# Differential attention on one core: scores two heads ahead, values one head behind, VectorE's work in a new order

## The reference, cut to what matters

```python
sc = jnp.einsum('bqhcd,bkhcd->bhcqk', qb, k)
p = jax.nn.softmax(sc, axis=-1)
a = p[:, :, 0] - lam_full * p[:, :, 1]
out = jnp.einsum('bhqk,bkhe->bqhe', a, v)
```

## Time and profile before

| | |
|---|---|
| Median of three runs | 3047.74 us (3039.37 to 3050.79) |
| The profiled execution | 3042.34 us |
| Its span in the trace | 3040.7 us |
| Granted clock of TensorE, mean | 0.917 of 2.4 GHz |
| TensorE matmul busy | 2671.5 us, 88% of the span |
| VectorE busy | 783.5 us, 26% |
| ScalarE busy | 336.9 us, 11% |
| GpSimd busy | 29.7 us, 1% |
| Moved by DMA | 729.65 MB, mean 240 GB/s |

### The profile page before, as it was taken

How to read it: one execution, slowest core, us unless ns; L and a number is a source line. 1 busy time by engine, 2 the same in 40 slices (tenths; PEclk the granted TensorE clock), 3 DMA queues, 4 the chain that set the end, 5 groups by cost and what they waited for, 6 DMA issues and landing times. The chain is left out here.

```text
span 3040.7 us, 28745 instructions
## 1 busy us (share of the span) xinstructions
PE 2671.5 (88%) x10935; PEld 1588.9 (52%) x10936; DVE 783.5 (26%) x1801; ACT 336.9 (11%) x663; POOL 29.7 (1%) x48
## 2 busy tenths in 40 slices
PE   6977699999997999968999799959998996957998
PEld 3433333333332333337787477647767774734775
DVE  1222322212121221232832243234441001232001
ACT  2111011111111111110122000010001000021000
POOL 0000000000000000000000000000000000000000
PEclk8967699999999999989999899969997997967999
DMA  7600599999998899966323477347963545102443
GB/s 296 242 0 2 229 419 428 428 429 428 428 428 342 349 428 428 428 265 234 139 100 149 152 288 260 111 148 259 354 225 132 166 154 196 57 1 83 152 136 105
DMA packets 188107, 729.65 MB, mean 240 GB/s; under 512 B 9343, under 2 KB 102877, under 8 KB 159381
## 3 DMA queue, kind: packets, MB, share of 16 engines
q1 hardware_dynamic: 169044, 653.41, 54.7%
q0 software_dynamic: 19008, 75.50, 6.5%
HBM read 727.83 MB, written 1.05 MB: 240 GB/s over the span
## 5 line engine op out<-in xcount | busy, mean ns | idle before, releaser
L2132 PE MATMUL bank<-hT,ffn_wgu 128*128 128x256 f32 x2816 | 622.3, 382 | 29.1 <-DMA ffn_wgu<-in_ffn_w_gu 25.8
L2132 PEld LDWEIGHTS bank<-hT,ffn_wgu 128*128 128x128 f32 x2816 | 538.7, 192 | 123.1 <-issue 42.8
L1387 PE MATMUL bank<-experts_raw,tiled_xs 128*64 128x512 f32 x2112 | 474.3, 599 | 17.4 <-DMA experts_raw<-in_w_up 13.6
L1387 PEld LDWEIGHTS bank<-experts_raw,tiled_xs 128*64 128x64 f32 x2112 | 147.8, 138 | 333.3 <-issue 295.1
L2146 PE MATMUL bank<-ffn_wd,ffn_actT 128*128 128x512 f32 x704 | 308.6, 592 | 0.0
L1387 PE MATMUL bank<-experts_raw,tiled_act_s 128*64 128x512 f32 x1056 | 241.0, 602 | 48.4 <-DMA experts_raw<-in_w_down 47.1
L1714 PE MATMUL bank<-hT,second_ring 128*128 128x256 f32 x1024 | 226.1, 384 | 17.2 <-DMA second_ring<-in_w_in 17.2
L1714 PEld LDWEIGHTS bank<-hT,second_ring 128*128 128x128 f32 x1024 | 197.4, 193 | 46.1 <-issue 18.5
L2195 DVE TENSOR_TENSOR ffn_actT<-ffn_silu,bank 128x256 f32<-128x256 f32 x88 | 36.9, 421 | 694.1 <-ACT ffn_silu L2175 694.1
L2146 PEld LDWEIGHTS bank<-ffn_wd,ffn_actT 128*128 128x128 f32 x704 | 133.8, 190 | 151.3 <-issue 149.2
L1387 PEld LDWEIGHTS bank<-experts_raw,tiled_act_s 128*64 128x64 f32 x1056 | 71.3, 137 | 196.1 <-issue 123.5
(11 more groups left out here) (460 smaller groups left out, 1974.2 us busy)
## 6 DMA issues: line engine op xcount, KB each, us to landing
experts_raw<-in_w_gate SPq DMA_DIRECT2D x64, 2048.0 KB, 23.7
experts_raw<-in_w_up SPq DMA_DIRECT2D x64, 2048.0 KB, 25.1
experts_raw<-in_w_down SPq DMA_DIRECT2D x64, 2048.0 KB, 25.5
ffn_wgu<-in_ffn_w_gu SPq DMA_DIRECT2D x88, 1024.0 KB, 9.8
ffn_side_w<-in_mod_w POOLq DMA_DIRECT2D x30, 2048.0 KB, 12.0
ffn_wd<-in_ffn_w_down SPq DMA_DIRECT2D x44, 1024.0 KB, 5.2
second_ring<-in_w_in SPq DMA_DIRECT2D x16, 2048.0 KB, 7.7
mla_wm<-in_w_mod SPq DMA_DIRECT2D x24, 1024.0 KB, 6.4
```

The source lines that it names most:

```text
L1387: last = nc.tensor.matmul(bank[b][h * HALF:(h + 1) * HALF, :], stationary(kt), raw[p][:, k, h * C:(h + 1) * C], start=kt == 0, stop=kt == ...
L2132: last = nc.tensor.matmul(bank[b][:, m * SEQ:(m + 1) * SEQ], wgu[:, s, m, k, f * P:(f + 1) * P], core.hT[:, k, :], start=k == 0, stop=k == ...
```

## The change

TensorE makes the scores of head h+2 before the transposes of head h, and the value product of head h-1 after them; `attend` is split into `turn_prob` and `attend`. On VectorE `finish` loses its copy of the output, which becomes `take_o`; the maxima of head h+2 come behind the finish of head h, and the copy of head h-2 between them. ScalarE's list is unchanged.

```diff
--- before.py
+++ after.py
@@ -2393,7 +2393,7 @@
                                                 qk[64 * c:64 * c + 64, KT + h, :], start=True, stop=True)
                     last.then_inc(*core.filled[b].up())
 
-            def attend(h):
+            def turn_prob(h):
                 b = 4 + h % 2
                 pe.wait_ge(*S["prob_ready"].next(pe, TT))
                 core.claim(pe, b)
@@ -2402,7 +2402,9 @@
                         last = nc.tensor.transpose(bank[b][:, c * SEQ + t * P:c * SEQ + (t + 1) * P],
                                                    prob[h % 2][:, t, 0, c * P:(c + 1) * P], core.ident[:])
                 last.then_inc(*core.filled[b].up())
-                core.copied(pe, b)
+
+            def attend(h):
+                core.copied(pe, 4 + h % 2)
                 b = 6 + h % 2
                 core.claim(pe, b)
                 for t in range(TT):
@@ -2414,10 +2416,14 @@
             pe.wait_ge(*S["turned"].next(pe, KT))
             core.copied(pe, 6, 7)
             scores(0)
+            scores(1)
             for h in range(H3):
-                if h + 1 < H3:
-                    scores(h + 1)
-                attend(h)
+                if h + 2 < H3:
+                    scores(h + 2)
+                turn_prob(h)
+                if h:
+                    attend(h - 1)
+            attend(H3 - 1)
             pe.wait_ge(*S["o_ready"].next(pe))
             for q in range(4):
                 core.claim(pe, q)
@@ -2545,16 +2551,23 @@
                                            ALU.mult, ALU.mult))
                     vec.scalar_tensor_tensor(p[:, t, 0, :], p[:, t, 0, :], soft[:, 3, i:i + 1], p[:, t, 1, :],
                                              ALU.mult, ALU.add).then_inc(*S["prob_ready"].up())
+
+            def take_o(h):
                 b = 6 + h % 2
                 dve.wait_ge(*core.filled[b].next(dve))
                 vec.tensor_copy(o[:, :, h * P:(h + 1) * P], bank[b][:, 0:SEQ].rearrange("p (t n) -> p t n", t=TT))\
                     .then_inc(*core.emptied[b].up())
 
             maxima(0)
+            maxima(1)
             for h in range(H3):
-                if h + 1 < H3:
-                    maxima(h + 1)
                 finish(h)
+                if h >= 2:
+                    take_o(h - 2)
+                if h + 2 < H3:
+                    maxima(h + 2)
+            take_o(H3 - 2)
+            take_o(H3 - 1)
             dve.wait_ge(*core.read(dve, 6))
             dve.wait_ge(*core.read(dve, 7))
             vec.tensor_copy(lam[:, 6:7], lam[:, 5:6]).then_inc(*S["mixed"].up())
```

## The result

The kernel with the change takes 3002.95 us in the median of four runs (2996.48 to 3005.73), against 3046.93 for the kernel before in four runs (3039.37 to 3050.79). The ratio of the runs is 0.9856, with a 95% interval of 0.983 to 0.9882: 1.4% faster.

What follows compares the result with a forecast made beforehand. In the heads no engine was full, so the order of work set the time. Heads 38.4 us shorter gave 3042.34 - 38.4 = 3003.9; set against the runs' median, 5.4 us above the profiled time: 3009 us, range 2999 to 3020.

Steps and rivals of the forecast that it cites:

- The ring: Heads: scores, maxima, finish, transposes and value product wait on each other in a circle, one turn of 9.49 us per head.
- VectorE's 3.82 us: Heads, new order: VectorE's work per head, maxima 1.53, finish 1.95 and copy 0.34 us, the bound at full clock.
- TensorE at half clock: Heads, new order: TensorE's work per head at 1.2 GHz, near 4.9 us, or 5.22 without overlap.
- the tail: End of the heads, last transposes to behind the last copy: 4.4 us, between 5.6 at half and 3.3 at full clock.
- filling the pipeline: Start of the heads: the pipeline's fill at low clock adds some 0.5 us, second transposes behind scores 2 and 3.
- The sum against the median: Whole kernel: profiled execution gave 3003.9 us; the runs' median was 5.4 us above the profiled time, so 3009 was set.
- Rival A: Heads: clock stays at 1.2 GHz and TensorE binds; 32.2 us gone, or 30.6; time 3015.5 to 3017; chance 0.24.
- B: Heads: the circle of waits still closes and pays 8.6 us per head; gain 6 us, time 3042; chance 0.05.
- C: Heads: a bank freed late holds the new order back, the stage keeps its 75 us; time 3048; chance 0.05.
- D: Behind the heads: half clock lasts through the output product into the next feed-forward; slower, 3085 us; chance 0.02.
- The output product's clock: Output product: where its clock rises may shift by 2 us either way, from 3.9 us at half clock now.
- The swinging clock: Heads: small idles between groups cycling over PSUM banks swing TensorE's clock; the gain would lie between 32.2 and 38.4 us.

Runs made afterwards that it cites:

- e3: The change with scores and maxima again one head ahead, late values and copies kept: heads 60.19 us, median 3027.53 us, ratio 0.9953 to the kernel before.
- e4: The change with VectorE taking the maxima of head h+2 before the finish of head h: heads 56.59 us, ratio 0.9939 to the kernel before.
- e5: The change with VectorE copying each head's output a second time, to scratch: heads 4.09 us apart, 35.52 us in all, 3006.02 us in one run.
- e6: The change with ScalarE instead of VectorE copying each head's output: heads 3.43 us apart, median 3000.17 us, ratio 0.9861 to the kernel before.
- e10: The change with 18 unused TensorE matmuls behind the last head: heads 33.71 us, 2995.63 us in one run.
- e2: The change with VectorE copying each head's output one head late instead of two: heads 50.96 us, median 3023.82 us, ratio 0.9933 to the kernel before.
- e7: The kernel before with seven unused TensorE matmuls per head ahead of the transposes: heads 59.84 us, median 3030.27 us, ratio 0.9962 to the kernel before.

## Why the prediction was right

It said 3009 us, 2999 to 3020, and faster at 0.93; the median is 3002.95.

- **The ring** was read rightly: e3 and e4 each close it again in one place and fall back to 8.4 us in the heads wholly at half clock, near the 8.6 that I worked out for such a ring.
- **VectorE's 3.82 us** a head measured 3.76; e5 and e6 move it by 0.33 either way, where I had put the copy at 0.34. The forecast of the transposes' wait, 1 us a head, is the 1.14 in the timeline.
- **TensorE at half clock**, 4.9 us: the new order never ran there long enough to show it. The rise that I expected a few us in came after the stretch at half clock shown above. TensorE's own work at full clock is 2.62 to 2.66 us a head, inside the 2.45 to 2.8 given.
- **The size of the gain** in the heads was 38.4 and is 40.7 us. The term that was off is the tail: I took 4.4 us, between 5.6 at half and 3.3 at full clock. It was 3.06 (2705.83 to 2708.89), since the clock stayed full. That was partly luck, and I had said that the clock there can be either: in e10, whose heads are the same code, the last four transposes take 1.11 us, at half clock, and the tail is 3.81 us (2699.87 to 2703.68). The other 0.9 lies ahead of the last transposes, 29.88 us behind the first maxima instead of 30.8. Half of it is the 0.5 us put down for filling the pipeline, which did not come up: the second transposes follow the first by 3.43 us, just VectorE's maxima and finish. The rest is 3.76 us a head in place of 3.82.
- **The sum against the median** carried the scatter: the profiled execution had been 5.4 us below the median of the runs, and now stands 2.8 above it. The execution time worked out from the profile, 3003.9, is nearer to the result than the 3009 that I set. Of the 6 us between 3009 and the median only 2.3 come from the heads; the rest lies in code that the change doesn't touch, and that scatters by as much.
- **The chances** were added up wrongly. With the forecast and A beyond the 15.2 us and B and C within, as the prediction has it, faster should stand at 0.88 and same at 0.10, not 0.93 and 0.05.
- **Rival A** (half clock throughout) did not happen, **B** and **C** neither; for **D**, the output product is the same as before.
- **The output product's clock** could shift by 2 us, I wrote; the study shows the two cases, 27.70 and about 29.65 us.
- **The swinging clock** of the Trainium skill was a rule against the change. A clock that changed its level showed in the orders that open the ring only in part (e2 to e4), not in the steady heads of this one.

## What to carry to other kernels

Where three engines hand a chain round and none is full, write down the ring and count how many heads one turn of it covers; a look-ahead that only one engine follows (e4), or that leaves one late reader in a queue (e2), gives back half of the gain. Once the ring is open, the engine with the most work per head sets the pace, and moving a single copy off it paid at every head (e6). The gaps on TensorE cost twice here, by themselves and by the clock, some 14 of the 40.7 us by e7, so the reordering is worth more than the waits that it removes.

## What the runs showed of the hardware

Transposes alone were followed by a rise of the clock. These are windows of e6 behind its heads; TensorE runs nothing but the 16 transposes of the norm in the first of them:

```profile
2714.50:2717.60 3.10, 2.65 (x13) 2.65 (x14) 1.79 (x5) 0.00 (x0) 0.00 (x0) 0.50 0.00 0
2718.00:2719.40 1.40, 0.26 (x3) 0.02 (x1) 1.22 (x2) 0.00 (x0) 0.00 (x0) 1.00 0.00 0
2719.60:2723.60 4.00, 4.00 (x10) 1.85 (x11) 0.00 (x0) 0.00 (x0) 0.00 (x0) 1.00 0.00 0
```

TensorE had idled for 9.00 us before them. At 2714.50 to 2717.60 it is at half clock with 13 transposes, and from 2718.00 on it has the full one, so that the output product begins at full speed. The Trainium skill, "TensorE: Matmul & The Clock Gate", "Part 4: PE-mode transpose", says that this work doesn't count for the clock as matmuls do; for these fp32 transposes the measurement differs from it, and decides. In the kernel before, the same idle time of 9.04 us and the same transposes were followed by half clock in the first 3.9 us of the output product. Whether a given execution starts its output product at full or at half clock I could not predict, and no run was made for it; the same code did both.
